# Late attention's values for two heads at once, another order of its maps, and roots of the differential norms by Newton steps on GpSimd

## The reference

```python
y_mla  = softmax(mask(q @ k.T * scale)) @ v                  # 8 latent heads, 512 tokens, causal
y_diff = rms_norm((p0 - lam * p1) @ v, subln_g) * (1 - lam_init)   # 4 differential heads: two softmaxes each, causal
y_mem  = softmax(q @ k_mem.T * scale) @ v_mem                # 4 memory heads, 256 memory tokens, no mask
x = x + (concatenate([y_mla, y_diff, y_mem]) * silu(z)) @ w_out
```

## Time and profile before

| | |
|---|---|
| median of 3 timed runs | 1072.48 us (1071.48 to 1075.55) |
| the profiled execution's own time | 1069.8 us |
| its span in the profile | 1068.0 us |
| granted TensorE clock, mean | 0.985 of full |
| busy over the span | PE 1025.1, DVE 608.9, ACT 542.2, POOL 408.4 us |

### The profile page before, as it was taken

One profiled execution on the slowest core, in us unless ns is written; L12 is line 12 of the kernel. 1 busy time (PEld: TensorE's weight loads), 2 busy tenths in 40 slices (PEclk: granted clock), 3 DMA queues, 4 the chain that ended last, 5 costly groups with the idle time before them and its releaser, 6 DMA issues.

```text
span 1068.0 us, 15096 instructions
## 1 busy us (share of the span) xinstructions
PE 1025.1 (96%) x5166; PEld 837.2 (78%) x5166; DVE 608.9 (57%) x1329; ACT 542.2 (51%) x1102; POOL 408.4 (38%) x211
## 2 busy tenths in 40 slices
PE   6999999999999999999999999999999989988798
PEld 3879888888778788888888888788887868756677
DVE  4547367988455566454545444433134989686732
ACT  5443666877434344444444443543334265977921
POOL 2456412000144443444444444414444244533332
PEclk8999999999999999999999999999999999989899
DMA  7564222111133323222222224343352224342213
GB/s 263 184 169 149 98 80 74 51 41 40 41 105 131 118 98 99 89 98 89 98 98 98 98 98 138 99 138 102 112 181 92 76 87 131 89 113 76 77 53 118
DMA packets 38812, 111.88 MB, mean 105 GB/s; under 512 B 5235, under 2 KB 8563, under 8 KB 38067
## 3 DMA queue, kind: packets, MB, share of 16 engines
q1 hardware_dynamic: 28572, 87.60, 25.2%
q10 hardware_dynamic: 8584, 18.89, 5.5%
q0 software_dynamic: 1600, 4.66, 1.2%
HBM read 100.25 MB, written 7.96 MB: 101 GB/s over the span
## 4 chain that ended last, share of the span: by engine, by line
issue 49%; PE 25%; POOL 15%; DVE 6%; ACT 3%; DMA 2%; POOLq 0%; ACTq 0%; DVEq 0%
POOL WLO L669 13%; PE PS L1877 7%; PE PS L1879 7%; PE PS L1878 7%; DMA RAW<-wstream 2%; PE PS L2228 1%; PE PS L2049 1%; PE PS L2077 1%; ACT WHI L744 1%; PE PS L2082 1%; DVE PB L1410 1%; DMA X<-xT 1%; DVE FX L1677 1%; DVE FX L1681 1%; DVE PB L1370 0%
## 5 line engine op out<-in xcount | busy, mean ns | idle before, releaser
L669 POOL TENSOR_TENSOR WLO<-RAW,WHI 128x1024 fp32r<-128x1024 f32 x147 | 355.8, 2421 | 576.4 <-ACT WHI L744 576.3
L744 ACT ACTIVATE WHI<-RAW 128x1024 fp32r<-128x1024 f32 x154 | 162.8, 1058 | 276.3 <-PE PS L1879 252.9
L1877 PE MATMUL PS<-HHI,WHI 128*128 128x512 f32 x648 | 256.8, 396 | 10.0 <-DVE HLO L1266 8.9
L1878 PE MATMUL PS<-HLO,WHI 128*128 128x512 f32 x648 | 254.0, 392 | 0.0
L1879 PE MATMUL PS<-HHI,WLO 128*128 128x512 f32 x648 | 253.9, 392 | 0.0
L1877 PEld LDWEIGHTS PS<-HHI,WHI 128*128 128x128 f32 x648 | 122.7, 189 | 40.1 <-issue 12.9
L1877 PE MATMUL PS<-BHI,WHI 128*128 128x512 f32 x368 | 145.4, 395 | 3.5 <-POOL WLO L669 2.0
L1879 PE MATMUL PS<-BHI,WLO 128*128 128x512 f32 x368 | 143.4, 390 | 0.0
L1878 PE MATMUL PS<-BLO,WHI 128*128 128x512 f32 x368 | 143.4, 390 | 0.0
L1879 PEld LDWEIGHTS PS<-HHI,WLO 128*128 128x128 f32 x648 | 122.7, 189 | 26.0
L1878 PEld LDWEIGHTS PS<-HLO,WHI 128*128 128x128 f32 x648 | 122.7, 189 | 25.4 <-issue 0.5
(11 more groups left out here) (334 smaller groups left out, 1503.6 us busy)
## 6 DMA issues: line engine op xcount, KB each, us to landing
RAW<-wstream SPq DMA_DIRECT2D x154, 512.0 KB, 3.2
X<-xT ACTq DMA_DIRECT2D x4, 512.0 KB, 9.2
BF<-wstream POOLq DMA_DIRECT2D x2, 1024.0 KB, 6.6
BG<-wstream POOLq DMA_DIRECT2D x2, 1024.0 KB, 7.0
bias_b<-bias_rows ACTq DMA_DIRECT2D x2, 1024.0 KB
FX<-bias_b ACTq DMA_DIRECT2D x8, 256.0 KB, 2.6
X<-xT ACTq DMA_DIRECT2D x8, 256.0 KB, 3.7
x_keep<-X ACTq DMA_DIRECT2D x2, 1024.0 KB, 6.4
```

Of the source, the lines that this page charges most:

```text
L669: pool.tensor_tensor(WLO[:, s, :], RAW[:, s, :], WHI[:, s, :].bitcast(F), ALU.subtract).then_inc(split_lo, 1)
L744: act.activation(WHI[:, c % 2, :], RAW[:, c % 2, :], ACT.Copy).then_inc(split_hi, 1)
L1877: pe.matmul(dst, a[0], b[0], start=first, stop=False, **kw)
L1878: pe.matmul(dst, a[0], b[1], start=False, stop=False, **kw)
```

## The change

- The values of two heads are computed together (`values_of_two`): for each block of 128 keys one matmul for the first head of a pair on its 64 columns and one for the second on the other 64, over all tokens that see the block. Nothing is done after the first head of a pair. Each pair has one PSUM bank, is gated, copied and split as one 128x512 tile.
- `LATE_ORDER` is new, so that the heads of a tile follow each other: maps 0 to 3 latent, 4 to 7 differential heads 0 and 1, 8 and 9 latent, 10 to 13 differential heads 2 and 3, 14 and 15 latent, 16 to 19 memory.
- ACT waits, before it copies a turned map of pair y, for the values of pair y-1 (`A["pv"]` at `m["y"]`); before, it waited for those of the head two back.
- The root of a norm: DVE makes mean plus eps and, instead of a reciprocal, a first guess by integer arithmetic on its bits; POOL does three Newton steps, twelve operations on 128x8, each waiting for the one before. ACT waits for it and only copies. The finishing step comes one iteration later (i - 5).
- The output projection's first unit takes the tiles 0 to 7 in order. It used to begin with 4 to 7 (differential and memory). The reload of YT comes one iteration later.

```diff
-        LATE_ORDER = [("mla", 0), ("mla", 1), ("diff", 0), ("mla", 2), ("mla", 3), ("diff", 1), ("mla", 4), ("diff", 2),
-                      ("mla", 5), ("diff", 3), ("mla", 6), ("mem", 0), ("mem", 1), ("mem", 2), ("mem", 3), ("mla", 7)]
+        LATE_ORDER = [("mla", 0), ("mla", 1), ("mla", 2), ("mla", 3), ("diff", 0), ("diff", 1), ("mla", 4), ("mla", 5),
+                      ("diff", 2), ("diff", 3), ("mla", 6), ("mla", 7), ("mem", 0), ("mem", 1), ("mem", 2), ("mem", 3)]
...
+        turned = [m for m in LATE if m["last"]]
+        for n, m in enumerate(turned):
+
+            m["y"], m["bank"], m["end"], m["mate"] = n // 2, 6 + n // 2 % 2, n % 2 == 1, turned[n - 1]
+        ENDS = turned[1::2]
...
+            def newton(tile):
+
+                x, y, t = SS[:, 0:8], SS[:, 8:16], SS[:, 16:24]
+                pool.wait_ge(dm_rin, tile + 1)
+                for n in range(3):
+                    chain.link(pool.tensor_tensor(t, y, y, ALU.mult))
+                    chain.link(pool.tensor_tensor(t, t, x, ALU.mult))
+                    chain.link(pool.tensor_scalar(t, t, -0.5, 1.5, ALU.mult, ALU.add))
+                    ins = pool.tensor_tensor(y, y, t, ALU.mult)
+                    if n < 2:
+                        chain.link(ins)
+                ins.then_inc(dm_root, 1)
...
+                if diff_tile(LATE, m["i"] - 3) is not None:
+                    newton(diff_tile(LATE, m["i"] - 3))
...
-                    tile = diff_tile(maps, i - 4)
+                    tile = diff_tile(maps, i - 5)
                     if tile is not None:
-                        act.wait_ge(dm_rin, tile + 1)
-                        act.activation(YSQ.rearrange("p (g e) -> p g e", g=8), SS[:, 0:8, None].broadcast_to([P, 8, 64]),
-                                       ACT.Sqrt).then_inc(dm_rstd, 1)
+                        act.wait_ge(dm_root, tile + 1)
+                        act.activation(YSQ.rearrange("p (g e) -> p g e", g=8), SS[:, 8:16, None].broadcast_to([P, 8, 64]),
+                                       ACT.Copy).then_inc(dm_rstd, 1)
...
-                        if m["n"] > 2:
+                        if name == "late" and m["y"]:
+                            act.wait_ge(A["pv"], m["y"])
+                        if name == "ab" and m["n"] > 2:
                             act.wait_ge(A["pv"], m["n"] - 2)
...
-                            act.activation(YT[rows, :], PS[rows, m["bank"], :], ACT.Copy).then_inc(A["y_hi"], 1)
-                            if m["h"] % 2:
-                                act.wait_ge(A["y_hi"], m["y"] + 1)
-                                act.activation(YSQ, YT, ACT.Square).then_inc(dm_sq, 1)
+                            act.activation(YT, PS[:, m["bank"], :], ACT.Copy).then_inc(A["y_hi"], 1)
+                            act.activation(YSQ, PS[:, m["bank"], :], ACT.Square).then_inc(dm_sq, 1)
...
-                            dve.tensor_tensor(ps[:, 0:256], PS[away:away + 64, m["bank"], 0:256], FX[rows, m["ztile"], 0:256],
-                                              ALU.mult)
-                            dve.tensor_tensor(ps[:, 256:512], ps[:, 256:512], FX[rows, m["ztile"], 256:512],
-                                              ALU.mult).then_inc(A["y_f"], 1)
+                        dve.wait_ge(A["pv"], m["y"] + 1)
+                        ps = PS[:, m["bank"], :]
+                        dve.tensor_tensor(ps, ps, FX[:, m["ztile"], :], ALU.mult).then_inc(A["y_f"], 1)
...
-                        dve.reciprocal(SS[:, 0:8], SS[:, 0:8]).then_inc(dm_rin, 1)
+                        dve.tensor_scalar(SS[:, 8:16].bitcast(I32), SS[:, 0:8].bitcast(I32), -0.5, float(0x5F3759DF),
+                                          ALU.mult, ALU.add).then_inc(dm_rin, 1)
...
+            def values_of_two(A, m):
+
+                pe.wait_ge(A["p_hi"], m["t1"])
...
+                for kb in range(m["nkb"]):
+                    q0, q1 = m["kb"](kb)
+                    for one in (m["mate"], m):
+                        own = one["rows"].start
+                        ins = pe.matmul(PS[own:own + 64, m["bank"], q0:q1], one["v"](kb)[:, own:own + 64],
+                                        turned_block(one, turned_slot("late", one), kb), start=kb == 0, stop=kb == m["nkb"] - 1,
+                                        skip_group_check=True)
+                ins.then_inc(A["pv"], 1)
...
-            dense("wout2", yo, y_out, [4, 5, 6, 7, 0, 1, 2, 3],
-                  {4: (A["biased"], LATE[-1]["g1"]), 6: (A["y_lo"], max(dm[8]["yf"], dm[9]["yf"])),
-                   7: (A["y_lo"], max(dm[10]["yf"], dm[11]["yf"])), 0: (A["y_lo"], max(m["yf"] for m in mla[:4])),
-                   2: (A["y_lo"], mla[5]["yf"]), 3: (A["y_lo"], mla[7]["yf"])})
+            dense("wout2", yo, y_out, range(8),
+                  {0: (A["y_lo"], mla[3]["yf"]), 2: (A["y_lo"], mla[5]["yf"]), 3: (A["y_lo"], mla[7]["yf"]), 4: (dm_lo, 2),
+                   6: (A["y_lo"], dm[9]["yf"]), 7: (A["y_lo"], dm[11]["yf"])})
```

More of the change, by code:

```diff
@@ L380, in build @@
                 m["n"] = n
-                if maps is LATE and not m.get("diff"):
+                if maps is LATE and m.get("end") and not m.get("diff"):
                     m["yf"] = 1 + len([n for n in maps[:i] if "yf" in n])
@@ L934, in attention @@
                             bias_load(m["bias"] + 1)
+                    if name == "late" and i == DIFF_AT[1] + 6:
+                        act.wait_ge(dm_lo, 2)
+                        act.dma_start(YT, r_keep).then_inc(r_in, 16)
                     if name == "ab" and 0 <= i - 2 < len(maps) and maps[i - 2]["last"]:
@@ L1443, in attention @@
                         ins.then_inc(cmp_lo, 1)
-                    tile = diff_tile(maps, i - 4)
+                    tile = diff_tile(maps, i - 5)
                     if tile is not None:
                         dve.wait_ge(dm_spread, tile + 1)
-                        dve.scalar_tensor_tensor(out=YT, in0=YT, scalar=col("subln"), in1=PS[:, DIFF_BANK[tile], :],
+                        dve.scalar_tensor_tensor(out=YT, in0=YT, scalar=col("subln"), in1=PS[:, SPREAD_BANK[tile], :],
                                                  op0=ALU.mult, op1=ALU.mult).then_inc(dm_read, 1)
@@ L1488, in attention @@
                         low_from_psum(lo(Y_DM + tile), hi(Y_DM + tile), YT).then_inc(dm_lo, 1)
-                    if name == "late" and 0 <= i - 2 < len(maps) and maps[i - 2]["last"]:
+                    if name == "late" and 0 <= i - 2 < len(maps) and "yf" in maps[i - 2]:
                         m = maps[i - 2]
[L1491 to L1495, removed]
-                            dve.tensor_tensor(ps[:, 0:256], PS[away:away + 64, m["bank"], 0:256], FX[rows, m["ztile"], 0:256],
-                                              ALU.mult)
-                            dve.tensor_tensor(ps[:, 256:512], ps[:, 256:512], FX[rows, m["ztile"], 256:512],
-                                              ALU.mult).then_inc(A["y_f"], 1)
+                        dve.wait_ge(A["pv"], m["y"] + 1)
+                        ps = PS[:, m["bank"], :]
+                        dve.tensor_tensor(ps, ps, FX[:, m["ztile"], :], ALU.mult).then_inc(A["y_f"], 1)
                     if diff_tile(maps, i - 3) is not None:
@@ L2055, in values @@
                 if m["first"] and y >= 2:
[L2056 to L2059, removed]
-                        if not before.get("diff"):
-                            pe.wait_ge(A["y_lo"], before["yf"])
-                        elif before["h"] % 2 and m["bank"] == DIFF_BANK[before["h"] // 2]:
-                            pe.wait_ge(dm_read, before["h"] // 2 + 1)
-                        else:
-                            pe.wait_ge(A["y_hi"], y - 1)
+                    pe.wait_ge(A["y_lo"], y - 1)
                 if m["first"] and name == "ab" and y > 8:
@@ L2070, in values @@
                     q0, q1 = m["kb"](kb)
-                    if name == "late" and not m.get("diff"):
-                        own = m["rows"].start
-                        v = m["v"](kb)[:, own:own + 64]
-                        p = turned_block(m, pt, kb)
-                        for half, c0, c1 in ((own, max(q0, 256), q1), (64 - own, q0, 256)):
-                            if c0 < c1:
-                                ins = pe.matmul(PS[half:half + 64, m["bank"], c0:c1], v, p[:, c0 - q0:c1 - q0],
-                                                start=kb == 0, stop=kb == m["nkb"] - 1 or c1 <= 256 and kb == 1,
-                                                skip_group_check=True)
-                        continue
-                    if name == "late":
-                        ins = pe.matmul(PS[:, m["bank"], q0:q1], m["v"](kb), turned_block(m, pt, kb), start=m["first"] and kb == 0,
-                                        stop=m["last"] and kb == m["nkb"] - 1, skip_group_check=True)
-                        continue
                     for half, qs in halves(m):
@@ L2108, in attention @@
```

(2 more changed lines are left out.)

49 lines of the change are left out of this document (29 added, 20 removed).

## The result

The changed kernel takes 1074.89 us, median of 20 runs (1072.65 to 1077.52), against 1072.13 (20 runs, 1070.40 to 1075.94) for the kernel before on the same chips: a ratio of 1.0025, 95% interval 1.0018 to 1.0033. It is 2.8 us slower, where 4.5 us less was predicted. The profiled execution took 1075.16 us, span 1073.3, against 1068.0 before.

A forecast was written before the change was run, and what follows sets the result against it. It took a chain between four in-order engines as the bound, no engine being full. The walk's 5.6 us gain less 1.1 for the clock gave -4.5: 1072.5 - 4.5 = 1068.0 us, range 1061 to 1077.

The forecast's parts named there:

- The walk: Late attention, each queue followed in program order at full clock: last values at 1011.2 instead of 1016.8, a gain of 5.6 us.
- Prices of single steps: Late attention, durations taken: causal pair 2.2 us, memory pair 1.8, PSUM product 0.70, GpSimd operation 0.30 with hand-over.
- DVE's and ACT's relief: Late attention, work taken off these engines: 10.3 us less of DVE, about 9.6 us less of ACT.
- The lock: Late attention, pairs fill both slots: ACT waits for the pair before, about 2.2 us at maps 2, 8, 14, 16, 18.
- 1.1 for the clock: Late attention, taken off the walk's gain: PE idles more, so low-clock stretches come somewhat oftener, 1.1 us.
- the 4.2 it left out before: Late attention of the kernel before: low clock and hand-overs, which the walk leaves out, worth 4.2 us.
- Rival D: Late attention: adjacent pairs meet half clock, 4.4 us instead of 2.2 with ACT behind them; +5.4, 1078; chance 0.10.
- rival C: Root on GpSimd: small operations cost 0.6 us each, 7.2 us a tile; +2.7, 1075; chance 0.15.
- 9.6 us of PE: Late attention, values computed in pairs: latent 4.4, differential 4.8, memory 0.4, together 9.6 us less of PE.
- The tail: Dense projection after the late attention: tile 7's low part, 2.2 us after the last values, and YT's reload stay hidden.
- B: Late attention: rival that the relief is paid in full, the stretch 9 us shorter; 1063.5; chance 0.27.

The follow-up runs named there:

- e1: Changed kernel with idle matmuls on PE in front of seven of its waits in the late attention: 1069.12 us, 0.9973 of the kernel before.
- e2: Changed kernel with a third slot for turned probabilities, two weight loads delayed for it: 1063.46 us, 0.9936 of the kernel before.
- e6: Changed kernel with the third slot and idle matmuls in front of three waits (maps 2, 7 and 12): 1063.75 us, 0.9941 of the kernel before.
- e5: Kernel before with one wait tightened: ACT's copy waits for the values of the head just before, not two back: 1080.62 us, 1.0086.
- e8: Changed kernel with two slots, only the two weight loads delayed until the last values: 1074.36 us, 1.0028 of the kernel before.
- e9: Kernel before with a third slot and single heads, ACT waiting for the head three back: 1072.42 us against 1070.90, 1.0010.
- e10: Changed kernel with the third slot and the root by ACT again with its table loads: 1070.35 us against 1070.90 of the kernel before, 0.9992.
- e4: Changed kernel with the root by ACT again, the later iteration kept: 1080.24 us, 1.0075 of the kernel before.
- e7: Kernel before with GpSimd's roots alone, without the one iteration more: 1075.59 us, 1.0031 of the kernel before.
- e3: Changed kernel with a pair's values moved ahead of the turning of the next map in PE's queue: 1074.32 us, 1.0026 of the kernel before.
- e11: Changed kernel with the third slot and a pair's values ahead of the next map's turning on PE: 1073.81 us, 1.0024 of the kernel before.
- e12: Third-slot kernel with the second tile's twelve GpSimd operations behind memory map 1's scaling instead of ahead: 1066.74 us, 0.9955 of the kernel before.

## Why the prediction was wrong

The walk can be held against the trace if both are counted from the scores of map 2 (922.6 in the walk, 925.00 in the trace):

| moment | walk, us | trace, us | behind |
|---|---|---|---|
| first pair begins | 11.7 | 11.9 | 0.2 |
| first pair done | 13.9 | 15.9 | 2.0 |
| differential pair 5, 7 done | 39.0 | 43.7 | 4.7 |
| first root done | 50.6 | 56.1 | 5.5 |
| pair 11, 13 done | 66.1 | 73.5 | 7.4 |
| pair 14, 15 done | 75.3 | 86.7 | 11.4 |
| last values done | 88.6 | 101.3 | 12.7 |

- **Prices of single steps: right.** A causal pair takes 2.31 us at full clock (2.2 taken), a memory pair 1.94 (1.8), the gating 0.70, a GpSimd operation 0.28 with its hand-over (0.30). DVE's and ACT's relief are within 1.1 us. No table load is left in the stage.
- **The lock: its mechanism right, its size wrong.** ACT waits for values at maps 2, 8, 14, 16 and 18, as the prediction said. It put the wait at "about 2.2 us" a pair, 11.0 for five. They sum to 19.1, and the long ones are 5.2 to 5.5, because ACT waits from the moment at which it is free, and PE comes late and slow. At full clock they still sum to 13.9 (e1).
- **The step that failed is the term "1.1 for the clock".** I reasoned on the mean of the stage. But the pairs don't stand anywhere in it: PE reaches most of them soon after idle time, in which it waited for the map ahead. Five of six ran at 0.50 to 0.65 and took 8.1 us more of PE's time, 5.0 of them with ACT standing still. Full clock gives back 5.8 us (e1), where 1.1 was counted: 4.7 of the miss. The walk lags by 12.7 us; the 4.2 it left out before and the 1.1 cover 5.3. The other 7.4 are the miss: -4.5 + 7.4 = +2.9, which is what the stage shows. The 2.7 us that the clock leaves are there at full clock too. The lock's 13.9 us for 11.0 are of that size, but e1's idle matmuls cost something as well, and no run tells the two apart.
- **Rival D named the mechanism**: it asked for two low pairs of the five ahead of which ACT waits, and three were low (the first, third and sixth causal pair; the fifth and the first memory pair ran at full clock). It had a chance of 0.10, though the prediction itself listed five low stretches and said that PE would idle more. Its price of 1078 took all five as low; with three it is -4.5 - 1.1 + 3 x 2.2 = +1.0, and 1.8 less than measured. The measured time lies in the band of rival C, whose mechanism did not happen.
- **How much of it is the clock, how much the lock** the runs tell in part: full clock with the lock gives 5.8 us (e1). No lock gives 9.5 to 11.4 (e2), with four of five low pairs gone too. With the lock gone and the first pair at full clock as well (e6) the time is 5.4 us below e1 by the medians, 3.4 by the ratios: about that much the lock costs by itself. Warming the first pair gives nothing once ACT doesn't wait for it (e6 against e2). So here the low clock cost time through the lock, as far as the pairs were warmed. The wait alone, with the low clock that it brought, costs 9.0 in the kernel before (e5), and neither the loads (e8) nor a slot as such (e9) is worth anything.
- **Even at full clock** the walk was too good: e1's stage takes 94.9 us for 88.6. What the walk leaves out (hand-overs, the lock's longer waits, and here the idle matmuls) is some 6 us, more than the 4.2 by which I corrected it from before, and e1 ends 2.3 us under before, not 4.5.
- **What pays inside the change** is not what I gave most to. I counted 9.6 us of PE, and the pairs with their order, freed of the lock, show no gain (e10, interval 0.9974 to 1.0011). Whether the pairs gain and the order loses as much was not told apart. GpSimd's root gives 5.3 us (e4) or 6.0 to 6.9 (e2 against e10). In the kernel before, at the old place, it costs 4.0 by the medians, 3.3 by the ratio (e7). ACT's 9.0 us of waiting there speak for the iteration more as a part of the gain; no run gave that iteration to the kernel before.
- **The tail: right.** The dense projection takes 47 us and no tile of its first unit waits. Rival C fell: 0.28 us, not 0.6. B fell, as the lock was not hidden. e2 comes to B's time, 1063.46, but not in its way: by e10 it is the root that pays, not PE's relief.

The direction was wrong. How much each of the five low pairs costs by itself is not settled: no run warmed a single one.

## What to carry to other kernels

When two steps are grouped into one, count the buffers in flight: a group that fills all slots locks producer and consumer to each other, and where two slots served single steps the group may need three (here 9.5 to 11.4 us). Price a step at the clock its engine has when it gets there, not at the stage's mean: soon after a wait it can be the low one (here in five of six pairs), and a locked neighbour pays it too. And before moving a step in a queue, look at what stands behind it: the values moved forward pushed the column sums back (e3, e11), the root moved back left an idle gap of 4.2 us empty (e12).

## What the runs showed of the hardware

- Twelve dependent GpSimd operations on 128x8 take 3.3 us, 0.20 each with a period of 0.28; once, in the changed kernel's first tile, 4.1 us with single operations up to 0.59.
- The two column halves of a pair run fully beside each other: 2 x 1280 columns in 2.31 us, as one full-width head before (2.32); at half clock 4.47, 1.94 times as much.
- The table load left no drain behind it in the profile, but taking away four, 5.1 us, gave 5.3 to 6.9. The Trainium skill ("ScalarE: Activation LUTs", What ACT_TABLE_LOAD costs) puts a drain of 1.38 us on each switch; an estimate from its figures for load and drain is 10.6 us for four. The runs lie between that and the loads alone, and what the rest of them is was not told apart.
